# First layer's attention: heads taken in pairs and four groups, woven with the query and output projections; weights through a ring of seven places

## The reference

```
for i in range(2):
    a = rmsnorm(h, norm_mix_pre[i])
    m = nsa_mixer(a, ...) if i % 2 == 0 else dilated_mixer(a, ...)
    h = h + rmsnorm(m, norm_mix_post[i])
    f = (silu(g) * u) @ w_down          # g, u = rmsnorm(h, ...) @ w_gu
    h = h + rmsnorm(f, norm_ffn_post[i])

# nsa_mixer: 16 query heads, 4 key/value heads, head size 64
proj = a @ w_in                          # q | k,v of cmp, sel, win | gates
kc = silu(blocks(k_cmp) @ wk1) @ wk2     # 15 blocks of 32 tokens; wk1 is 2048x256
vc = silu(blocks(v_cmp) @ wv1) @ wv2
o_cmp = softmax(q . kc) . vc             # no rotation
o_sel = softmax(rope(q) . rope(k_sel)) . v_sel
o_win = softmax(rope(q) . rope(k_win)) . v_win
o = g0*o_cmp + g1*o_sel + g2*o_win ;  return o @ w_o
```

## Time and profile before

| | us |
|---|---|
| median of 3 runs | 866.75 |
| the execution that was profiled | 868.74 |
| span in its profile | 867.0 |
| TensorE busy | 845.7 (98%) |
| VectorE busy | 535.7 (62%) |
| ScalarE busy | 478.5 (55%) |
| GpSimd busy | 37.5 (4%) |

### The profile page before, as it was taken

The page is one execution under the profiler, slowest core; times in us unless marked ns, Lnnn a source line. Parts: engine busy times, 40 slices in busy tenths (PEclk is TensorE's granted clock), DMA queues, the critical chain, the costliest instruction groups (busy, mean ns, idle before and its releaser), DMA issues.

```text
span 867.0 us, 12254 instructions
## 1 busy us (share of the span) xinstructions
PE 845.7 (98%) x4345; PEld 682.6 (79%) x4345; DVE 535.7 (62%) x1136; ACT 478.5 (55%) x862; POOL 37.5 (4%) x120
## 2 busy tenths in 40 slices
PE   6999999989999999999999999999999999999996
PEld 5898666778888888877887888888777888888885
DVE  5978786586655554577546554655556955555544
ACT  7777666664544444464555655655566754444431
POOL 3000028200000000000000000000000000000000
PEclk9999999999999999999999999999999999999999
DMA  7667100273665556529654354354331657645611
GB/s 261 214 194 244 53 2 1 66 226 110 206 221 167 191 184 206 163 90 306 200 189 144 102 180 158 103 175 158 124 122 51 219 194 227 208 152 187 220 69 48
DMA packets 108958, 137.35 MB, mean 158 GB/s; under 512 B 6336, under 2 KB 92400, under 8 KB 108784
## 3 DMA queue, kind: packets, MB, share of 16 engines
q1 hardware_dynamic: 107824, 132.53, 47.6%
q0 software_dynamic: 992, 4.19, 1.5%
q10 hardware_dynamic: 96, 0.02, 0.0%
HBM read 134.64 MB, written 2.10 MB: 158 GB/s over the span
## 4 chain that ended last, share of the span: by engine, by line
PE 90%; DVE 4%; DMA 3%; ACT 2%; issue 1%; SPq 0%; ACTq 0%; DVEq 0%
PE ps L1557 76%; PE ps L1566 5%; PE ps L1750 3%; PE ps L1781 3%; DVE w_lo L1085 2%; PE ps L1773 1%; ACT w_hi L618 1%; DMA w_raw<-in_dil_w_in 1%; DMA w_raw<-in_ffn_w_gu 1%; DMA h<-in_x 1%; PE ps L1800 1%; PE ps L1728 0%; DVE xt_lo L1117 0%; ACT junk L639 0%; SPq L425 0%
## 5 line engine op out<-in xcount | busy, mean ns | idle before, releaser
L1085 DVE TENSOR_TENSOR w_lo<-w_raw,w_hi 128x1024 fp32r<-128x1024 f32 x248 | 297.3, 1223 | 133.9 <-ACT w_hi L618 132.0
L1557 PE MATMUL ps<-w_hi,xt_hi 128*128 128x512 f32 x760 | 308.9, 406 | 2.9 <-DVE xt_lo L1117 2.4
L1557 PE MATMUL ps<-w_hi,xt_lo 128*128 128x512 f32 x760 | 299.2, 394 | 0.0
L1557 PE MATMUL ps<-w_lo,xt_hi 128*128 128x512 f32 x760 | 298.2, 392 | 0.0
L618 ACT ACTIVATE w_hi<-w_raw 128x1024 fp32r<-128x1024 f32 x248 | 254.8, 1057 | 38.8 <-DMA w_raw<-in_ffn_w_gu 21.4
L1557 PEld LDWEIGHTS ps<-w_hi,xt_hi 128*128 128x128 f32 x760 | 144.5, 190 | 32.3 <-DVE xt_lo L1117 2.9
L1557 PEld LDWEIGHTS ps<-w_hi,xt_lo 128*128 128x128 f32 x760 | 144.1, 190 | 31.6
L1557 PEld LDWEIGHTS ps<-w_lo,xt_hi 128*128 128x128 f32 x760 | 144.6, 190 | 27.0
L883 ACT ACTIVATE st_hi<-ps 128x256 fp32r<-128x256 f32 x40 | 15.3, 383 | 102.3 <-PE ps L1566 102.1
L1557 PE MATMUL ps<-w_hi,st_hi 128*128 128x512 f32 x160 | 62.6, 391 | 0.0
L1557 PE MATMUL ps<-w_hi,st_lo 128*128 128x512 f32 x160 | 62.3, 389 | 0.0
(11 more groups left out here) (206 smaller groups left out, 853.5 us busy)
## 6 DMA issues: line engine op xcount, KB each, us to landing
w_raw<-in_ffn_w_gu SPq DMA_DIRECT2D x88, 512.0 KB, 4.7
w_raw<-in_dil_w_in SPq DMA_DIRECT2D x72, 512.0 KB, 4.6
w_raw<-in_ffn_w_down SPq DMA_DIRECT2D x44, 512.0 KB, 4.2
w_raw<-in_nsa_w_in SPq DMA_DIRECT2D x20, 512.0 KB, 4.6
w_raw<-in_nsa_w_o SPq DMA_DIRECT2D x8, 512.0 KB, 4.9
w_raw<-in_dil_w_o SPq DMA_DIRECT2D x8, 512.0 KB, 3.6
w_raw<-in_nsa_cmp_wk SPq DMA_DIRECT2D x4, 512.0 KB, 4.9
w_raw<-in_nsa_cmp_wv SPq DMA_DIRECT2D x4, 512.0 KB, 4.1
```

Of the source, the lines that this page charges most:

```text
L1085: dve.tensor_tensor(w_lo[:, n.slot, c:c + 1024], w_raw[:, n.raw, c:c + 1024], w_hi[:, n.slot, c:c + 1024].bitcast(F32), ALU.subtract)\
L1557: ins = pe.matmul(o, s, m, start=start, stop=stop)
```

## The change

- **Pairs.** `pair_nsa` takes two heads (16 pairs in four groups of four: heads 0 to 7 with m = 0, the same with m = 1, then heads 8 to 15). Both heads' scores are matmuls over 64 partitions each, from one copy of the keys (`k_both`; `k_z` and its zeroing on GpSimd go). There are two score banks, so `scores_nsa(s)` waits until pair s-1 is masked. Values go to both halves of the output partitions in turn; the compressed branch is four matmuls at a group's end. For m = 0 the probabilities of both heads are turned together.
- **Norm.** Per pair one reciprocal, one multiplication with the gates and one `tensor_tensor` over 2 heads x 2 branches, in place of a reciprocal per unit and a `tensor_scalar` per branch.
- **Weave.** Query tiles 8 and 9 and the output projection are cut into steps of 3 or 6 matmuls (`q_part`, `o_nsa`), which stand between the attention's steps on TensorE. On ScalarE and VectorE the weight splits of pieces 13 to 18 stand between them in halves. `turn_q` is written into fewer banks, and `qu_t` holds half as many heads.
- **Compression.** `compress` uses fp32 weights and blocks uncut (32 matmuls of 256 columns, those of k and v on the two halves of the output partitions); the splits of four pieces and of the blocks go.
- **Ring.** Seven places; raw weights are loaded where `w_lo` will stand and are subtracted in place. A load waits until TensorE has used the piece seven before; a split waits for the load alone.
- **Start.** The rows of gains come in two parts; x's second half is turned in the middle of tile 0; ScalarE's first table is loaded by an activation of its own.
- **Loops** in `ffn` are unrolled. One turn in the second layer (`dil_turn` of tile 3) is moved behind tile 4.

The diff, cut to its core:

```diff
-RAW = 2
-RING = 6
+RING = 7
@@ load
-                    if pc.n0 >= RAW and not (pc.woven and k):
-                        sp.wait_ge(lo_ready, pc.halves(2 if pc.woven else k + 1) - 2 * RAW)
+                    if pc.n0 >= RING and k == 0:
+                        sp.wait_ge(piece_used, pc.n0 - RING + 1)
@@ scalar
+            def attend(s):
+                k, m = turns_nsa(s - 1) if s else 0, pair_nsa(s)[1]
+                if s:
+                    pt_out_nsa(k)
+                if s < PAIRS_NSA:
+                    exp_unit(0, 2 * s, P * (m + 1), 2)
+                if s and pair_nsa(s - 1)[1]:
+                    pt_out_nsa(k + 1)
+                if s < PAIRS_NSA:
+                    exp_unit(0, 2 * s + 1, P * (m + 1), 2)
...
+            attend(4)
+            split(13)
+            cmp_turned(0)
+            ot_hi_nsa(0)
+            attend(5)
+            turn_q(1, 0, 3, 2)
+            proj_evac(q_rows)
+            split(14, (0,))
+            attend(6)
+            split(14, (1,))
+            turn_q(1, 1, 3, 2)
+            attend(7)
+            split(15, (0,))
+            attend(8)
+            cmp_exp(1)
+            ot_hi_nsa(1)
+            attend(9)
+            split(15, (1,))
+            attend(10)
+            cmp_turned(1)
+            split(16, (0,))
+            attend(11)
+            split(16, (1,))
+            attend(12)
+            ot_hi_nsa(2)
+            split(17, (0,))
+            attend(13)
+            split(17, (1,))
+            attend(14)
+            split(18, (0,))
...
+            attend(15)
+            post_squares(1, 0)
+            attend(16)
+            ot_hi_nsa(3)
@@ vector
+            def norm_nsa(s):
+                r, m, j = pair_nsa(s)
+                n, at = P * (m + 1), s % 2 * 2
+                r_pair = rl[:, at:at + 2, :]
+                dve.wait_ge(expd[0], 2 * s + 2)
+                link(dve.reciprocal(r_pair, l_u[:, at:at + 2, :]))
+                link(dve.tensor_tensor(r_pair, r_pair, view(gates, ...), ALU.mult))
+                p = view(probs, at * 512, [[512, 2], [n, 2], [1, n]])
+                dve.tensor_tensor(p, p, view(rl, at * 2, [[2, 2], [1, 2], [0, n]]), ALU.mult).then_inc(normed[0], 1)
...
+            mask_nsa_pair(4)
+            rope(0, 9, stage_rot, 0, 8, 0)
+            split(13)
+            norm_nsa(4)
+            ot_lo_nsa(0)
+            mask_nsa_pair(5)
+            rope(0, 10, stage_rot, 1, 8, 1)
+            norm_nsa(5)
+            mask_nsa_pair(6)
+            split(14)
+            norm_nsa(6)
+            mask_nsa_pair(7)
+            split(15, (0,))
+            norm_nsa(7)
+            mask_nsa_pair(8)
+            cmp_scores(1)
+            norm_nsa(8)
+            ot_lo_nsa(1)
+            mask_nsa_pair(9)
+            cmp_probs(1)
+            split(15, (1,))
+            norm_nsa(9)
+            mask_nsa_pair(10)
+            split(16, (0,))
+            norm_nsa(10)
...
@@ tensor
+            def scores_nsa(s):
+                r, m, j = pair_nsa(s)
+                n = P * (m + 1)
+                if s:
+                    pe.wait_ge(masked[0], 2 * s)
+                for odd in range(2):
+                    hd, rows = 8 * r + 2 * j + odd, slice(DH * odd, DH * odd + DH)
+                    pe.matmul(bank(score_bank(odd), 0, 2 * n), q_t[rows, hd // 2, m * P:(m + 1) * P],
+                              k_both[rows, :, hd // G, 0:n], start=True, stop=True).then_inc(scores[0], 1)
...
+            q_part(9, (3,))
+            cmp_turn(0)
+            q_part(9, (4,))
+            compressed_nsa(0)
+
+            scores_nsa(5)
+            q_part(9, (5,))
+            probs_nsa(4, 0)
+            q_part(9, (6,))
+            probs_nsa(4, 1)
+            q_part(9, (7,))
+            turn_q(6, 0, 3, 2)
+            values_nsa(4)
+
+            scores_nsa(6)
+            o_nsa(0, 0, 0)
+            probs_nsa(5, 0)
+            o_nsa(0, 0, 1)
+            probs_nsa(5, 1)
+            o_nsa(0, 0, 2)
+            values_nsa(5)
...
+            scores_nsa(10)
+            o_nsa(1, 0, 1)
+            probs_nsa(9, 0)
+            cmp_turn(1)
+            o_nsa(1, 0, 2)
+            values_nsa(9)
...
+            probs_nsa(15, 0)
+            probs_nsa(15, 1)
+            values_nsa(15)
+            compressed_nsa(3)
+
+            o_nsa(1, 0, 4, 5, 6, 7)
+            turn_h0(1, 0)
+            o_nsa(1, 1, 4, 5)
+            turn_h0(1, 1)
+            o_nsa(1, 1, 6, 7)
```

More of the change, by code:

```diff
@@ new lines, in _ @@
+            proj_evac(q_rows)
+            turn_kv(1, 1, 5)
+            split(11)
+            turn_q(0, 0, 7, 2)
+            hid_less()
+            attend(0)
+            split(12)
+            proj_evac(q_rows)
+            attend(1)
+            kc_blocks()
+            turn_q(0, 1, 1, 2)
+            attend(2)
+            attend(3)
+            cmp_exp(0)
+            proj_evac(q_rows)
+            attend(4)
[3 more added lines that the diff above has]
+            attend(5)
@@ L1247, in _ @@
[L1247 to L1256 removed]
+            split(7)
@@ new lines, in _, with hid_silu @@
+            rope(0, 5, stage_nsa, 0, 2 * HK, 0)
+            rope(0, 6, stage_nsa, 1, 2 * HK, 1)
+            split(10)
+            rope(0, 7, stage_rot, 0, 8, 0)
+            split(11)
+            def hid_silu():
+                dve.wait_ge(hid_exp, 1)
+                link(dve.tensor_scalar(e_hid[:, :], e_hid[:, :], 1.0, None, ALU.add))
+                link(dve.reciprocal(e_hid[:, :], e_hid[:, :]))
+                dve.tensor_tensor(hid_r[:, :], bank(3, 0, 256), e_hid[:, :], ALU.mult).then_inc(hid_ready, 1)
@@ L1615, in _, with turn_x @@
             pe.wait_ge(ident_ready, 1)
-            for m in range(MT):
+            pe.wait_ge(rows_loaded[0], 16)
+            pe.transpose(bank(2, 0, 16), rows[0][:, :], ident[0:16, 0:16]).then_inc(rows_t, 1)
+            def turn_x(m):
                 pe.wait_ge(x_loaded[m], 16)
@@ new lines, in compressed_nsa @@
+            def compressed_nsa(g):
+                r, m = divmod(g, 2)
+                if m == 0:
+                    pe.wait_ge(pct_out, r + 1)
+                    pe.wait_ge(vc_out, 1)
+                for j in range(4):
+                    hk = 2 * r + j // 2
+                    ins = pe.matmul(bank(OT_BANK, P * j, P), vc_bd[:, hk, j % 2 * P:j % 2 * P + P],
+                                    pc_t[:, 2 * hk + m, :], start=False, stop=True, skip_group_check=True)
+                ins.then_inc(pv_done[0], 1)
@@ new lines, in turn_h0 @@
+            def turn_h0(b, half):
+                pe.wait_ge(h_ready[b][half], 1)
+                xt_turn(b, 0, half, h)
+            compress(range(8))
+            pe.wait_ge(turn_out[0], 2)
+            turn_q(4, 0, 7, 2)
+            compress(range(8, 16))
+            pe.wait_ge(turn_out[0], 5)
+            scores_nsa(0)
+            q_part(7, range(8))
+            scores_nsa(1)
+            q_part(8, (0,))
+            hid_turns()
+            q_part(8, (1,))
+            probs_nsa(0, 0)
```

816 lines of the change are left out of this document (393 added, 423 removed).

## The result

The changed kernel takes 879.04 us (median of four, 878.53 to 879.86): 1.0137 times the kernel before, 95% interval 1.012 to 1.0153. That is 12 us above the kernel before and above the forecast of 867, and 1.0 above the top of the range. The profiled execution took 878.89 us with a span of 877.1, 10.1 more than the one of before.

What follows compares the result with a forecast made beforehand. TensorE, busy 98% of the span, was taken to bound the kernel: 868.7 - 36.6 (work) + 5.3 (weave) + 33.1 (waits) - 3.2 - 0.7 + 2.5 (clock) = 869.1 profiled, so 867 us forecast, range 848 to 878.

Steps and rivals of the forecast that it cites:

- the clock: Around TensorE's waits in attention: four or five falls to 1.2 GHz, +2.5 us (0 to +8).
- the last step of the forecast: Whole kernel: 869.1 us for the profiled execution, lowered to 867 because the old profiled execution was 2.0 above its median.
- The forecast's own walk: Attention's end after pair 15: nothing covers the second turning, values, copy and remainder, a wait of 2.9 us.
- Compression: Compression on TensorE: 16 pairs of 256 fp32 columns at 0.45, 7.2 us, 4.4 saved (3.1 to 4.8).
- The chain: Attention pairs with a split: closed chain across TensorE, ScalarE and VectorE, 7.55 us for m = 1, 6.2 for m = 0.
- The wait ahead of the first compressed values: Pair 4: TensorE waits 3.3 us for `cmp_turned(0)`, which stands behind exponentials and split 13 on ScalarE.
- The ring: Feed-forward weight loads: issued at least 5.6 us ahead of their split, so 0 (to +4 if late).
- One sign that the forecast named: Start of feed-forward part: its first matmul should start within 3 us of the old 192.1.
- Shorter chain: Attention pairs: chain links overlap by 1.2 us per pair over ten pairs, 12 us faster, 855; chance 0.20.
- waits covered: Attention: waits largely covered, TensorE's own sum decides, 837 us; chance 0.10.
- late loads: Feed-forward steps: loads gated by use come late, 16 at 0.5 us, 875; chance 0.05.
- Low clock: Attention from pair 4: repeated waits keep TensorE at 1.2 GHz in over half the m = 1 steps, +14, 881; chance 0.15.

Runs made afterwards that it cites:

- The two halves of the fill: Changed kernel with useless matmuls in TensorE's waits only at the attention's end, 874.64 us, or only in the pairs, 871.38 us.
- the kernel with filled waits: Changed kernel with useless matmuls in TensorE's waits in the pairs from pair 5, ahead of the first compressed values and at the attention's end: 868.20 us.
- the half-filled one: Changed kernel with half as many useless matmuls at the same waits (four, six and three instead of eight, twelve and six): 868.82 us.

## Why the forecast was wrong

**The failed term is the clock: +2.5 forecast, 10.8 measured.** The forecast took four or five falls at about 0.6 us each, and there were five. It went wrong on two steps. It priced a fall by the one in the trace before, 3.4 us long with 1.7 lost; here they last 3.4 to 13.7 us, 37.5 in all. And it let the slow work fill the next wait. That holds where a wait follows (0.2 and 0.5 us lost with the spells at 146 and 167), and fails where none does, or where the slow work itself is awaited: around the first compressed values (2.9 lost), between pairs 7 and 8 (2.7), where `compressed_nsa(1)`, the scores with the compressed keys and a projection step fill TensorE without a gap, and in the end (4.4), where turning, values and remainders are the chain. The forecast's own walk named that end as uncovered (2.9) and did not price it at 1.2 GHz. The two halves of the fill place the cost there and in the pairs.

**Of the 12.0 us by which the forecast missed, the clock is 8.3.** Another 2.1 come from the last step of the forecast, which took off 2.0 because the profiled execution of the kernel before lay 2.0 above its median; that of the changed kernel lay 0.15 below its own. The remaining 1.6 are sums of small terms.

**The rest of the sum held, in part by luck.** Without the clock term the forecast for the profiled execution is 866.6; the kernel with filled waits took 867.5 in its profiled execution, 0.9 more. By stretches, its start was 0.3 later than before, where 0 (-1.5 to +1) was forecast. From the end of tile 5 to the feed-forward part it was 0.3 shorter than before, where 2.1 was forecast. From there to the end it was 1.3 shorter, where 0 was forecast. The last two errors, 1.8 and 1.3, mostly cancel.

- Scores of a pair took 1.06 and 0.63 (forecast 1.07 and 0.53 to 0.55), values 1.02 and 0.59, turnings of four blocks 0.35 to 0.41.
- Compression took 3.6 + 3.6 = 7.2 us for 16 pairs of matmuls, as forecast. Each matmul leaves two records; a record of k and one of v, on the two halves of the output partitions, start 0.01 apart, and the next such two come 0.215 later. So a pair of matmuls takes 0.43 within a row, less than the 0.53 of one matmul with 256 columns among other shapes. That is the changed kernel's timeline:

```profile
59.33 0.43 PE L1568 MATMUL ps<-w_k,tb 128*64 128x256 f32 x1
59.34 0.43 PE L1568 MATMUL ps<-w_raw,tb 128*64 128x256 f32 x1
59.60 0.38 PE L1568 MATMUL ps<-w_k,tb 128*64 128x256 f32 x1
```

- The chain: 7.53, 7.54, 7.58 and 7.59 measured (8.26 with a spell), 7.55 forecast; m = 0: 6.1 to 6.7, 6.2 forecast. The nine splits are worth 17.0 us; 18 was expected.
- The wait ahead of the first compressed values: 2.44 in the trace, 3.3 forecast.
- The ring: 0 forecast; `w_hi` waits 0.4 us for loads in the whole kernel.
- One sign that the forecast named failed: the first feed-forward matmul was to start within 3 us of the old 192.1. It starts at 205.0 in the changed kernel, and at 193.9 with all waits filled.

**The rivals.** "Shorter chain" and "waits covered" are out by the turnings' distances, "late loads" by the 0.4 us. "Low clock" gave 881, and its time is nearest, but not by its mechanism: it wanted more than half of the m = 1 steps at the low clock, each longer by 2.8, and of the five with a split four are 7.53 to 7.59 long, as at full clock. That the measured 879 lies near its 881 is a coincidence. The section of the Trainium skill (TensorE: Matmul & The Clock Gate, "HAM oscillation — how this bites in real kernels") tells of a kernel in which every burst between waits started at the half rate. Here the trace agrees in part: the clock does fall around waits, but in five spells, 37.5 of the 102 us from the first to the last of them, and most steps ran at full rate. The truth lay between forecast and rival: few falls, as in the one, but long ones on uncovered work, which neither priced.

## What to carry to other kernels

A weight split that is moved into attention must stand where its engine waits anyway: behind the mask, and not between exponentials and norm. In this kernel the same nine splits cost 17 us more in the one place than in the other; with that and two smaller moves in the same queues the change gains 2.0% instead of losing 1.4%.

When work is taken from TensorE and the gaps are not closed, price the gaps twice: as waits, and as low clock on whatever TensorE does next without a gap. Where no real work fits, a few useless matmuls in the wait are a cheap test of which it is.

## What the runs showed of the hardware

- The granted clock fell for 3.4 to 13.7 us at a time, in or shortly after waits of 1.7 to 2.7 us, and in the end of the attention it stayed down while waits of 0.7 to 1.7 us alternated with work. With half of each wait filled, the mean clock was 0.994 to 0.996 in six of ten executions and 0.982 to 0.991 in four; with all of it filled it was 0.997 to 0.999 in every one.
- One microsecond at 1.2 GHz cost 0.29 us in the changed kernel and 0.41 us between executions of the half-filled one, both on average: by place it was from 0.05 (the spell at 146) to 0.4 (the one at 98).
- Two fp32 matmuls of 256 columns with 64 output columns each, on different halves of the output partitions, ran together: 0.43 us for both (two records each, 0.215 apart).
- One `tensor_tensor` of 1024 columns with a broadcast operand took 1.27 us, four `tensor_scalar`s of 256 took 1.42.
